# Sparse attention by pairs of units, both pairs of heads of a group next to each other on a query block

## The reference, cut to what matters

```python
s = einsum('bqgrd,bngd->bgrqn', qb, kc)                 # 31 compressed keys
p_cmp = where(vis, softmax(where(vis, s, NEG)), 0.0)
o_cmp = einsum('bgrqn,bngd->bqgrd', p_cmp, vc)
...
s = where(ok, einsum('bqgrd,bgqkld->bgrqkl', qb, kg), NEG)   # selected blocks
o_slc = einsum('bgrqkl,bgqkld->bqgrd', softmax(s), vg)
...
s = einsum('bqgrd,bkgd->bgrqk', qb, kw)                      # window of 512
o_win = einsum('bgrqk,bkgd->bqgrd', softmax(where(band, s, NEG)), vw)
o = g0 * o_cmp + g1 * o_slc + g2 * o_win
```

## Time and profile before

| | us |
|---|---|
| median of 3 runs | 3334.95 (3333.59 to 3335.91) |
| the profiled execution | 3336.66 |
| its span | 3334.9 |
| mean granted TensorE clock | 0.985 of full |
| the sparse stage in the span | 2726.9 to 2933.16 |

### The profile page before, as it was taken

One profiled execution on the slowest core, in us unless ns is written; L12 is line 12 of the kernel. 1 busy time (PEld: TensorE's weight loads), 2 busy tenths in 40 slices (PEclk: granted clock), 3 DMA queues, 4 the chain that ended last, 5 costly groups with the idle time before them and its releaser, 6 DMA issues. The chain is left out here.

```text
span 3334.9 us, 48578 instructions
## 1 busy us (share of the span) xinstructions
PE 3172.2 (95%) x19852; PEld 1896.4 (57%) x19852; DVE 1873.8 (56%) x3335; ACT 1304.4 (39%) x2349; POOL 81.4 (2%) x148
## 2 busy tenths in 40 slices
PE   6999989999999999999999998999999999999998
PEld 3576756756666556746655465364445555564444
DVE  5237667665634555766576466663334558863334
ACT  3234444434432324444445344343223236743322
POOL 0000001100000000001000000000000000000000
PEclk8999999999999999999999999999999989999999
DMA  7311111031122221111221332223223310023222
GB/s 302 152 52 39 39 43 39 31 95 39 40 95 82 94 79 53 39 68 36 65 88 62 118 114 89 76 76 114 102 85 118 118 57 1 1 79 112 101 91 86
DMA packets 48908, 264.17 MB, mean 79 GB/s; under 512 B 6024, under 2 KB 9736, under 8 KB 28080
## 3 DMA queue, kind: packets, MB, share of 16 engines
q1 hardware_dynamic: 48112, 257.92, 22.2%
q10 hardware_dynamic: 576, 3.15, 0.2%
HBM read 254.66 MB, written 4.19 MB: 78 GB/s over the span
## 5 line engine op out<-in xcount | busy, mean ns | idle before, releaser
L313 PE MATMUL banks<-h_sb,wsplit_sb 128*128 128x512 f16 (+2 forms) x8256 | 1576.2, 347 | 50.0 <-PEq L86 13.8
L313 PEld LDWEIGHTS banks<-h_sb,wsplit_sb 128*128 128x128 f16 x8256 | 799.1, 98 | 787.5 <-issue 115.0
L298 DVE SCALAR_TENSOR_TENSOR wsplit_sb<-ring_sb,wsplit_sb 128x1024 f16<-128x1024 f32 (+2 forms) x428 | 471.1, 1115 | 429.4 <-ACT wsplit_sb L288 426.8
L288 ACT ACTIVATE wsplit_sb<-ring_sb 128x1024 f16<-128x1024 f32 (+2 forms) x428 | 405.0, 962 | 615.7 <-PE banks L313 598.0
L313 PE MATMUL banks<-quads,wsplit_sb 128*128 128x512 f16 (+2 forms) x3300 | 590.1, 337 | 4.4 <-PEq L86 4.4
L313 PEld LDWEIGHTS banks<-quads,wsplit_sb 128*128 128x128 f16 x3300 | 321.7, 98 | 255.2 <-issue 11.1
L313 PE MATMUL banks<-wsplit_sb,h_sb 128*128 128x256 f16 x2112 | 240.1, 274 | 0.0
L313 PEld LDWEIGHTS banks<-wsplit_sb,h_sb 128*128 128x128 f16 x2112 | 207.1, 98 | 31.3 <-issue 6.0
L532 ACT ACTIVATE quads<-banks 128x256 f32<-128x256 f32 (+2 forms) x214 | 98.6, 463 | 306.0 <-PE banks L313 305.6
L619 PE MATMUL banks<-quads 64*128 64x256 f32 (+3 forms) x432 | 111.9, 504 | 19.6 <-DVE W_sb L1417 12.6
L1641 ACT ACTIVATE work_sb<-banks 128x768 f32<-128x768 f32 (+1 forms) x80 | 57.9, 724 | 172.0 <-PE banks L1652 131.4
(11 more groups left out here) (335 smaller groups left out, 3181.3 us busy)
## 6 DMA issues: line engine op xcount, KB each, us to landing
ring_sb<-in_w_in SPq DMA_DIRECT2D x52, 1024.0 KB, 4.8
ring_sb<-in_w_ffn SPq DMA_DIRECT2D x44, 1024.0 KB, 4.8
ring_sb<-in_w_merge SPq DMA_DIRECT2D x48, 768.0 KB, 4.4
ring_sb<-in_w_ffn SPq DMA_DIRECT2D x32, 704.0 KB, 4.0
quads<-in_w_mod SPq DMA_DIRECT2D x12, 1024.0 KB, 26.1
x_sb<-in_w_mod SPq DMA_DIRECT2D x12, 1024.0 KB, 7.1
ring_sb<-in_w_ab SPq DMA_DIRECT2D x12, 1024.0 KB, 5.1
ring_sb<-in_w_nsa SPq DMA_DIRECT2D x10, 1024.0 KB, 4.8
```

The source lines that it names most:

```text
L288: act.activation(m.wsplit[:, s, 0, half * n:half * n + n], m.ring[:, s, half * n:half * n + n], ACT.Copy, scale=WSCALE).then_inc(w.hi[s], 1)
L298: dve.scalar_tensor_tensor(m.wsplit[:, s, 1, half * n:half * n + n], m.ring[:, s, half * n:half * n + n], WSCALE, m.wsplit[:, s, 0, half * ...
L313: mm = pe.matmul(p.bank, *p.terms(k, pw, px), start=(p.opens and k == 0 and z == 0), stop=(p.closes and k == p.depth - 1 and z == 2))
```

## The change

All of it is in `sparse_window`. The units are ordered so that both pairs of heads of a group take the same query block one after the other: t goes 0, 0, 3, 3, 1, 1, 2, 2 by pairs. On TensorE both units of a pair come next to each other in scores and in values. The other due times move with it, those of the compressed tiles too, which are now spread over the round of 16 units. The maxima write the bias themselves: the reduction multiplies the masked score by -1/8 and takes the minimum, the exponential has the scale -1, the scaling instruction and both waits of VectorE on its own steps go. `maxed` counts heads in place of units, so a head's exponential waits for that head alone. One wait of the compressed copy is renumbered for the new order.

```diff
-    units = [(g, rp, t, j) for g in range(NG) for rp in range(2) for t in order for j in range(2)]
+    units = [(g, rp, t, j) for g in range(NG) for t in order for rp in range(2) for j in range(2)]
...
-    cmp_at = lambda i: -4.0 + 6.5 * i if i < 4 else at(16 * (i // 4 - 1), 8.3 + 3.0 * (i % 4))
+    cmp_at = lambda i: (-4.0, 2.5, 9.0, 17.0)[i] if i < 4 else at(16 * (i // 4 - 1), 9.3 + 4.0 * (i % 4))
...
         def scores(pe):
-                yield at(u, 0.0)
+                yield at(u - j, 0.4 + 0.01 * j)
                 nk = (t + 1) * P
                 if u >= 2:
-                    pe.wait_ge(maxed, u - 1)
+                    pe.wait_ge(maxed, 2 * (u - 1))
...
         def maxima(dve, step):
-                yield at(u, 0.45)
+                yield at(u, 0.9 - 0.2 * j)
...
                 for c in range(2):
-                    step(dve.tensor_tensor_reduce(E[u % R][:, c, 0:nk], ps[:, 2 * (u % 2) + c, 0:nk], mask[:, S - nk:S], 1.0, -3.0e38,
-                                                  ALU.add, ALU.max, x[:, c:c + 1]))
-                dve.tensor_scalar(x[:, 2:4], x[:, 0:2], -SCALE64, None, ALU.mult).then_inc(maxed, 1)
+                    dve.tensor_tensor_reduce(E[u % R][:, c, 0:nk], ps[:, 2 * (u % 2) + c, 0:nk], mask[:, S - nk:S], -SCALE64, 3.0e38,
+                                             ALU.add, ALU.min, x[:, 2 + c:3 + c]).then_inc(maxed, 1)
...
         def exps(act):
-                yield at(u, 0.95)
+                yield at(u, 1.35 - 0.1 * j)
-                act.wait_ge(maxed, u + 1)
                 for c in range(2):
+                    act.wait_ge(maxed, 2 * u + c + 1)
                     act.activation(E[u % R][:, c, 0:nk], E[u % R][:, c, 0:nk], ACT.Exp, bias=x[:, 2 + c:3 + c],
-                                   scale=SCALE64, accum_out=x[:, 4 + c:5 + c]).then_inc(exp_done, 1)
+                                   scale=-1.0, accum_out=x[:, 4 + c:5 + c]).then_inc(exp_done, 1)
...
         def weights(dve, step):
-                yield at(u, 1.75)
+                yield at(u, 2.0)
...
         def values(pe):
-                yield at(u, 4.0)
+                yield at(u - j, 5.4 + 0.01 * j)
...
         def outs(act):
-                yield at(2 * p + 1, 4.6)
+                yield at(2 * p + 1, 5.0)
...
         def lows(dve):
-                yield at(2 * p + 1, 5.2)
+                yield at(2 * p + 1, 5.6)
...
         def cmp_act(act):
-                    act.wait_ge(valued, 16 * (i // 4 - 2) + 8 + 2 * (i % 4) + 1)
+                    act.wait_ge(valued, 16 * (i // 4 - 2) + 4 * (i % 4) + 3)
```

## The result

The changed kernel took 3349.17 us (median of 4, 3346.13 to 3353.56) against 3334.95 before: 14.2 us slower, ratio over the runs 1.0036, 95% interval 1.0024 to 1.0048 (the two medians alone give 1.0043). 3325.0 was forecast. The profiled execution has a span of 3349.7 us.

What follows compares the result with a forecast made beforehand. VectorE (44.8 us a round) was the bound by a hair over TensorE (43.9). First round 4.5 + two steady rounds 3.4 + last units 1.5 + tail 0.6 = 10.0 us: 3334.95 becomes 3325.0, range 3318.5 to 3333.

Steps and rivals of the forecast that it cites:

- The maxima edit: VectorE's maxima: scaling and two waits removed, saving 0.19 to 0.20 us a unit, 12.8 us over 64 units (5 to 20).
- rival of unchanged handovers: VectorE's handovers stay at 0.12 us, leaving it 43.5 us a round; total 3328.5 us; chance 0.10.
- The order step: Steady rounds in the new unit order: 46.0 us in place of 47.67, 3.4 us less for two.
- slot sum: Steady round: larger of TensorE's and VectorE's time in each pair slot, summed: 46.8 us new order, 46.3 before.
- the loss of before: Steady round: the 1.35 us by which the old order's measured 47.67 exceeded its summed 46.3.
- edit 2: ScalarE's exponentials wait per head, the first starting 0.3 to 0.7 us earlier; priced at nothing by itself.
- The ends of my range: Steady round between 43.9 us (TensorE with perfect overlap) and 48.15 us (as much loss as before).
- Bunching: Rival: grouping equal sizes eats the steady gain, round 47.7 to 48.15 us, 3 us gained, total 3332; chance 0.16.
- TensorE's floor: Steady rounds: TensorE's own 43.9 us busy as the lower bound of a round.
- The scores at the head of the queue: Rival: unreleased odd scores idle TensorE in 32 pairs; gain gone from 0.31 us a pair; 3344 at 0.6; chance 0.09.
- The first round: First 16 units, 61.0 us before: near 56.5 us with less waiting for compressed scores, 4.5 us saved (3 to 6).
- low clock: TensorE at 0.50 of its clock, 1.2 GHz, for at least 15 us of the first round; spreading there would disprove the forecast.

Runs made afterwards that it cites:

- maxima only: Kernel before with only the maxima rewrite and the exponentials' wait per head, unit order and due times as before; ratio 0.9976, stage 199.7 us.
- output later: Changed kernel with copies due at 3.2 in place of 3.3, outputs at 5.5 and low parts at 6.1; ratio 0.9993, stage 204.9 us.
- pairs only, copy first: Kernel before with the maxima rewrite and seven new due times, mixed sizes, copies due at 3.2 in place of 3.3; 3322.63 us, ratio 0.9954.
- pairs only: Kernel before with the maxima rewrite and seven new due times (pairs adjacent on TensorE), unit order and compressed due times as before; ratio 0.9976.
- pairs only, copy late: Kernel before with the maxima rewrite and seven new due times, mixed sizes, copies due at 3.6 in place of 3.3; ratio 0.9981.
- order only, copy first: Changed kernel with the maxima, scaling and waits of before, and copies due at 3.2 in place of 3.3; ratio 1.0016, stage 205.6 us.
- the filler: Twenty unread 128x128 TensorE transposes a round, added before scores of units 2, 4, 6, 8: changed kernel ratio 1.0036, "pairs only" 0.9994.

## Why the prediction was wrong, by its own steps

**The maxima edit was under-sized.** I took 0.06 us for a handover behind an accumulator read, and saved 0.19 to 0.20 us a unit. VectorE's timeline of the changed kernel answers to the earlier trace rows:

```profile
2861.71 0.68 DVE L2632 CUSTOM_DVE_ANT_0 work_sb<-banks,GB_sb 128x512 f32<-128x512 f32 x1
2862.32 0.08 DVE L2632 DVE_READ_ACCUMULATOR2_ANT small_sb<- 128x1 f32 x1
2862.32 0.68 DVE L2632 CUSTOM_DVE_ANT_0 work_sb<-banks,GB_sb 128x512 f32<-128x512 f32 x1
2862.93 0.08 DVE L2632 DVE_READ_ACCUMULATOR2_ANT small_sb<- 128x1 f32 x1
2862.93 0.16 DVE L2650 RECIPROCAL small_sb<-small_sb 128x2 f32<-128x2 f32 x1
```

The next instruction starts with the read, both times: 0.31 us saved a unit, the upper bound that I had named. That is 5 us of VectorE's time a round, and "maxima only" shows 2.1 of it reaching the round. The rival of unchanged handovers is refuted, and with it the Trainium skill's rule (VectorE: DVE Perf Modes, "The DRAIN you can't avoid") as far as it says that waits between VectorE operations cost nothing: here each cost 0.11 to 0.12 us. The same section excepts a next operation that is not held; whether the ones behind these reads are such, no run here tests.

**The order step failed.** I wrote that a round would take 46.0 us, the middle between TensorE's 43.9 and the slot sum plus the loss of before, and of ScalarE only, under edit 2, that "it is off the bound, so I price it at nothing by itself". The slot sums held VectorE and TensorE alone, though TensorE already waited 3.4 us a round for ScalarE's copies. ScalarE is busy 32.8 us of 51.2, but its queue is in order, and with four units of t = 3 together a copy that TensorE needs stands behind exponentials of t = 3. VectorE's waits, forecast near 4 us a round, came to 11.1, half of them for compressed scores. Moving 0.1 in its due time took 13.9 us off the stage, more than the 9.3 us by which it had grown (21.9 against 14.2 by the medians). So it is shown that the copy's place costs more than the whole slowdown. Not all of this cost came with the new order: with sizes mixed the same move takes 6.9 us off the stage, 8.8 by the medians. The ends of my range were wrong too: 48.15 was no upper bound, because it assumed that a loss of the new order would be the loss of the old one.

**Bunching is real beside it.** With the copy first and the pairs adjacent in both, mixed sizes take 190.7 us, grouped sizes 201.8; by the medians the difference is 8.9 us. A round of "output later" without any low clock takes 46.6 us, one of "pairs only, copy first" without any takes 43.3. So 3.3 us a round are left to the grouping at the full clock (the due times of the output and of the compressed tiles differ between the two as well). The slot sums had put the grouping at 0.5 us (46.8 against 46.3; as printed the slots sum to 46.7), because they let nothing wait but one engine for the other. I gave the rival 0.16.

**TensorE's floor was mis-sized.** I took 43.9 us as a bound below. Both units of a pair together cut it to 41.3. Part of the reason could be read before: the weight load stood idle for 0.17 us ahead of every block of values, and with pairs together there are half as many blocks. The first row is from the second round of "maxima only", the second from that of "pairs only":

```profile
PEld banks L2696 <- issue: 2.7, 16, 0.2
```

```profile
PEld banks L2696 <- issue: 1.4, 8, 0.2
```

I saw such rows in the trace of before and did not count them.

**The scores at the head of the queue**, my rival on the slower side, are not it: TensorE waited 4.5 us for maxima in the whole stage (1.0 before), 0.14 us a pair, under the 0.31 at which the gain was to be gone.

```profile
PEld banks L2620 <- DVE small_sb L2632: 4.5, 13, 0.7
```

**The first round** was forecast at 56.5 and took 57.5. The last fifteen units, forecast at 37.9, took 41.6, and the tail, forecast at 9.9, took 12.9. In the tail TensorE waits once for 2.0 us for a copy, and the clock of 0.92 in the last fifteen units is 6.7 us at the low level. These are places where I had counted busy time only.

**The clock.** I named a low clock in the first round only; it came in every round. How much of a round it costs was not separated. Some rounds of one execution run the same instructions with and without it: "output later" 46.6 us at 1.00 and 46.7 at 0.96, "pairs only, copy late" 45.4 at 1.00 and 46.9 at 0.96, "order only, copy first" 47.2 at 1.00 and 48.8 at 0.93, "pairs only, copy first" 43.3 at 1.00 and 43.8 at 0.96. That is 0.1 to 1.6 us of round for 3 to 7 us of low clock. The records that lengthen with it (TensorE busy 45.9 us in the changed kernel's third round, 41.7 in the round of "output later" that has the same unit order and no low clock) say about 4.2 us. So it is part of the loss, and which of the two, waits or low clock, starts the other in a given round stays open: the filler did not settle it, and of the two low stretches in the third round, which begin at 2858.6 and 2868.9, only the second follows the 1.75 us wait.

## What to carry to other kernels

When an order is changed, walk every in-order queue through the new order, the one of the engine with the lowest load too: what counts is what stands ahead of the instruction that another engine waits for, and how long that is now. Grouping work of equal size can make this worse, since the largest pieces then queue behind each other. A gain and a loss in one change are worth running apart: here either half of the order, beside the maxima edit, was no slower than before, and one due time of 3.2 in place of 3.3 turned 0.36% slower into 0.27% faster. A profile is one execution: where two variants are compared by it, the medians belong beside it, as they took most of the difference between 32.9 and 13.9 us away.

## What the runs showed of the hardware

- An accumulator read on VectorE with no wait behind it holds the engine for nothing that can be seen: the next instruction starts at the same time stamp (2862.32 and 2862.93).
- The time ahead of the stage, for the same instructions, ran from 2710.3 to 2723.0 us between executions, as the low-clock time in it ran from 54.6 to 81.9 us. The kernel before had looked steady to 0.07% in its first three runs; on other chips its own runs spread from 3332.3 to 3344.8 us.
- Twenty extra 128x128 transposes a round, 2.5 us of work, cost 3.0 us in "pairs only", and the granted clock fell there from 1.00 to 0.96.
